# One filler product ahead of the scores in the first steps of each attention stage

## The reference, cut to what matters

```python
logits = jnp.einsum('bqhe,bkhe->bhqk', q, k) * (dh ** -0.5) + bias
p = jax.nn.softmax(jnp.where(mask, logits, -inf), axis=-1)
o = jnp.einsum('bhqk,bkhe->bqhe', p, v)
```

## Time and profile before

| | |
|---|---|
| median of 3 runs | 2877.5 us (2838.91, 2877.5, 2881.47) |
| profiled execution, its own time | 2876.28 us |
| its span, first to last instruction | 2874.5 us |
| TensorE busy | 86% of the span |
| mean granted TensorE clock | 0.888 of full speed |

### The profile page before, as it was taken

One profiled execution on the slowest core, in us unless ns is written; L12 is line 12 of the kernel. 1 busy time (PEld: TensorE's weight loads), 2 busy tenths in 40 slices (PEclk: granted clock), 3 DMA queues, 4 the chain that ended last, 5 costly groups with the idle time before them and its releaser, 6 DMA issues. The chain is left out here.

```text
span 2874.5 us, 31094 instructions
## 1 busy us (share of the span) xinstructions
PE 2486.3 (86%) x11173; PEld 1916.7 (67%) x11173; DVE 1060.6 (37%) x2010; ACT 949.1 (33%) x1428; POOL 349.4 (12%) x367
## 2 busy tenths in 40 slices
PE   4797786998689989689999789977996998799999
PEld 2586574566378868478878578933554786588877
DVE  4835522343454432332222312175335333322222
ACT  1222111333345532244421222274235332344311
POOL 0001310221022210011100000022123000111100
PEclk6897885989889999899999899886588999899999
DMA  7850001002023323033332232101001332133321
GB/s 265 268 145 15 1 1 38 5 23 59 29 85 96 96 85 90 29 88 95 95 97 79 63 90 82 49 4 44 1 30 30 88 99 76 59 95 96 112 83 67
DMA packets 347878, 212.18 MB, mean 74 GB/s; under 512 B 20252, under 2 KB 327122, under 8 KB 347757
## 3 DMA queue, kind: packets, MB, share of 16 engines
q1 hardware_dynamic: 342848, 202.64, 23.9%
q10 hardware_dynamic: 4942, 8.43, 0.8%
HBM read 208.35 MB, written 9.24 MB: 76 GB/s over the span
## 5 line engine op out<-in xcount | busy, mean ns | idle before, releaser
L220 PE MATMUL ffn_up_psum<-ffn_h_hi,ffn_up_w_hi 128*128 128x512 f32 x704 | 275.8, 392 | 35.3 <-DVE ffn_up_w_lo L299 35.3
L221 PE MATMUL ffn_up_psum<-ffn_h_lo,ffn_up_w_hi 128*128 128x512 f32 x704 | 275.3, 391 | 0.0
L222 PE MATMUL ffn_up_psum<-ffn_h_hi,ffn_up_w_lo 128*128 128x512 f32 x704 | 275.2, 391 | 0.0
L299 DVE TENSOR_TENSOR ffn_up_w_lo<-ffn_up_raw,ffn_up_w_hi 128x1024 fp32r<-128x1024 f32 x88 | 107.7, 1226 | 340.4 <-ACT ffn_up_w_hi L295 340.4
L220 PEld LDWEIGHTS ffn_up_psum<-ffn_h_hi,ffn_up_w_hi 128*128 128x128 f32 x704 | 133.2, 189 | 64.5 <-DVE ffn_up_w_lo L299 37.0
L295 ACT ACTIVATE ffn_up_w_hi<-ffn_up_raw 128x1024 fp32r<-128x1024 f32 x88 | 93.1, 1060 | 198.9 <-PE ffn_up_psum L222 195.9
L220 PE MATMUL conv_up_psum<-h_hi,conv_up_w_hi 128*128 128x512 f32 x352 | 137.9, 392 | 22.1 <-DVE conv_up_w_lo L299 22.1
L221 PEld LDWEIGHTS ffn_up_psum<-ffn_h_lo,ffn_up_w_hi 128*128 128x128 f32 x704 | 133.2, 189 | 27.8
L222 PEld LDWEIGHTS ffn_up_psum<-ffn_h_hi,ffn_up_w_lo 128*128 128x128 f32 x704 | 133.0, 189 | 27.7
L220 PE MATMUL ffn_down_psum<-ffn_hidden_hi,ffn_down_w_hi 128*128 128x512 f32 x352 | 139.4, 396 | 13.2 <-DVE ffn_down_w_lo L299 13.2
L221 PE MATMUL ffn_down_psum<-ffn_hidden_lo,ffn_down_w_hi 128*128 128x512 f32 x352 | 138.7, 394 | 0.0
(11 more groups left out here) (581 smaller groups left out, 5567.9 us busy)
## 6 DMA issues: line engine op xcount, KB each, us to landing
conv_up_raw<-in_ffn_up_dram SPq DMA_DIRECT2D x44, 512.0 KB, 3.7
ffn_up_raw<-in_ffn_w_gate_dram SPq DMA_DIRECT2D x44, 512.0 KB, 3.7
ffn_up_raw<-in_ffn_w_up_dram SPq DMA_DIRECT2D x44, 512.0 KB, 3.7
ffn_down_raw<-in_ffn_w_down_dram SPq DMA_DIRECT2D x32, 704.0 KB, 4.5
in_a_mod_slots<-in_ada_w_dram SPq DMA_DIRECT2D x16, 1024.0 KB, 6.7
branches_raw<-in_w_in_dram SPq DMA_DIRECT2D x24, 512.0 KB, 3.6
down_raw<-in_ffn_down_dram SPq DMA_DIRECT2D x16, 704.0 KB, 4.7
mod_slots<-in_ada_w_dram SPq DMA_DIRECT2D x4, 2048.0 KB, 14.0
```

The costliest lines, as they stand in the source:

```text
L220: pe.matmul(out, w_hi, r_hi, start=start, stop=False)
L221: pe.matmul(out, w_hi, r_lo, start=False, stop=False)
L222: return pe.matmul(out, w_lo, r_hi, start=False, stop=stop)
L299: dve.tensor_tensor(self.lo[:, j % PAIRS], self.raw[:, j], self.hi[:, j % PAIRS].bitcast(F32), ALU.subtract)\
```

## The change

In every step from the fifth on (i of 4 or more) and below `weigh_lag` + 2, PE gets one more product after its wait for the bias and ahead of the score. It multiplies the identity with the first columns of the constant matrices, writes them to the bank that the score is about to fill, and nobody reads them. In fox, nsa, sel and diff these are steps 4 to 8, five products a stage; in dil they are steps 4 to 10, seven. That makes 27. The first four steps have none.

```diff
+def filler_columns(score):
+
+    keys = 0 if score is None or score.coarse else score.keys
+    lacking = 0.85 * max(600 + 0.95 * keys, 750 + 0.8 * keys) - max(60, 2 * keys / 2.4)
+    return min(int(lacking * 2.4 / 4) // 32 * 32, T // 2)
+
...
                     u, c, x = pieces[i]
                     if i >= 4:
                         pe.wait_ge(biased, i - 3)
+                        filler = filler_columns(x)
+                        if i < weigh_lag + 2:
+                            pe.matmul(psum[:, i % 4, 0:filler], attention.ident,
+                                      flat(attention.square[:, 0:TT])[:, 0:filler], start=True, stop=True)
                     cols = slice(x.lo * P, x.lo * P + x.keys)
```

## The result

| | runs | median us | lowest to highest |
|---|---|---|---|
| changed kernel | 4 | 2911.74 | 2895.37 to 2918.14 |
| kernel before, beside it | 4 | 2860.01 | 2838.91 to 2881.47 |

The ratio is 1.019, with a 95% interval of 1.0119 to 1.0261: slower, by 1.2 to 2.6%. 2839 us was forecast. The profiled execution took 2895.37 us, its span is 2893.6.

A forecast was written before the change was run, and what follows sets the result against it. PE was taken to bound every attention stage, so a clock fall costs nearly its full length; 2876.3 + 6.8 (fox, sel, diff) + 3.8 (nsa) - 47.6 (dil) = 2839 us, range 2822 to 2853, or 2822 to 2889 with rivals.

The forecast's parts named there:

- The base: Starting time of the sum: the profiled execution of the kernel before, 2876.3 us, with dil's mean clock at 0.55.
- dil, the front: Dil's steps 4 to 10: seven fillers cut the 2.00 us wait for POOL to 0.4, costing +1.5 us.
- dil, the clock: Dil from its first transposes: if the full clock holds, 55.1 us gained less 6 of new waits, 49.1 us.
- Rival B: Dil: clock held at the front, lost at the first, second or third slot's end; 2863 us, chance 0.17.
- nsa: Nsa: five fillers at half clock, 4.6 us less 0.80 of wait, +3.8 us; ends +1 and 6.0.
- fox, sel, diff: These three stages: all 15 fillers on PE's path at 0.46 us each, less 0.15: +6.8 us, ends 0 and +9.0.
- A: Rival in dil: the clock falls at the stage's start all the same; 2889 us, chance 0.20.
- C: Rival in dil: transposes don't hold the clock, which falls near 1980; 2885 us, chance 0.03.

The follow-up runs named there:

- before_again: The kernel before, unchanged, run again for a second profile: median 2841.77 us against 2841.84 for the kernel before on the same chip.
- the lean kernel: Kernel before plus ten wide fillers in dil alone, in steps 4 to 7 and two at each of three slots' ends: 2833.89 us, ratio 0.990 to 0.998.
- the longer start: Kernel before without fillers, but with four warm-up products instead of three in nsa: median 2852.95 us against 2841.30.
- nsa_step8_only: Kernel before plus one filler, in step 8 of nsa: median 2913.60 us against 2841.30, with nsa at 151.9 us in its profile.
- fox_sel_diff: Kernel before plus the change's 15 fillers in fox, sel and diff alone: median 2850.50 us against 2841.84.

## Why the prediction was wrong

*The size of it.* The profiled run lies 56.1 us over the sum: 37.6 in dil, 13.9 in nsa, 2.5 in fox, sel and diff, 2.1 outside these stages. The median lies 16.4 higher still.

*The base.* The sum started from 2876.3 us, a run whose dil was at half clock for 126 us. Before's usual run has 31 us of it (13.7 and 17.1), and a median of 2841.8. I had seen 2838.91 among three runs, and wrote that a dil that kept its clock would explain it; before_again's profile, at 2838.07, shows just that, but I gave it no weight in the sum. This didn't put the number off; it hid that most runs of before had little left to gain. The gain open in dil was 144.0 - 99.9 = 44 us from the profiled run and only 7 from the usual one.

*dil, the front*: right. 2.00 us became 0.45 (0.4 was said), and the clock didn't fall there, in any of the five profiles with wide fillers at dil's front; it fell at 10.6 to 10.7 us in all eight without fillers there. One reading was wrong: I put the second wait of the earlier trace rows, 0.7 us, beside the fillers of steps 8 to 10. It stands at dil's end, at 2099.53.

*dil, the clock*: the largest error, wrong in its condition "if it holds". 49.1 us were counted on a clock that holds to dil's end. It held for 34.1 us and was then at half for 92.2, so that dil gained 10.0 in all where 47.6 was forecast. Rival B (0.17) came true at the first of its three places: the fall at 2022.96, just behind the wait of 0.64 at the slot's end. The size was about right: with the clock held dil is 99.9 to 102.9, 41 to 44 us less than 144.0. New waits take 6.6 us in the lean kernel and 6 were put down, but that is luck: I charged them to POOL at every unit's end, and it is 1.6 us for POOL in two waits and 5.0 for ACT's copies in seven.

*nsa*: the step that failed without a rival. "+3.8 us" priced the fillers and left the return where it was, but for a sooner one. The stage was at half clock for 34 us more, which with the fillers' own length cost 17.7, three times the upper end of 6.0. I took the return at 603.6 for something that the stage's work brings about on its own; it was one lucky place, and the longer start shows that even 0.85 us destroys it. B alone would have given 2876, inside the range; with nsa's late return on top the time left it.

*fox, sel, diff*: right that all 15 lie on the path. The term was mis-sized: 0.46 each was said, and 0.58 (by the median) to 0.62 (by the stages' lengths) measured, at the upper end of 0.6. The diff row that I used has equal products back to back; the filler stands between unlike ones. That the load of the weights makes the difference is likely and not shown. ACT isn't free for half of the time in diff, as I wrote: it is busy for 28.28 of 54 us. Nothing came of that.

*A* (0.20) didn't happen in the profiled run. The three other runs of the changed kernel took 2905.66 to 2918.14, 10 to 23 us over it, and have no profile; which stage took these stays open. An nsa of 151.9 us, as with the one filler in step 8, in place of 129.0 would give 2918.3, near the two slowest; that is a guess. *C* is not borne out: the lean kernel's dil ran all its transposes at 1.00. The Trainium skill's advice in TensorE: Matmul & The Clock Gate, "Why this matters for your kernels", is to leave no idle gap of some microseconds between matmul bursts. The traces don't follow the length of the gap: the clock fell behind waits of 0.64 and 0.66 us and held through waits of 1.1 us in the lean kernel.

## What to carry to other kernels

Where a stage's clock can settle in two ways, take several profiles before costing an edit, and cost it against the usual one. Any delay, even of useless work, moves everything behind it, and a return of the clock that came by luck may not come again; so guard the places where PE's work is thin (a wait, a run of small products) and no others, and read the granted clock of every stage behind the edit. In fox, sel and diff, where PE was already full, the fillers bought nothing and cost their length. A place that is thin loses the clock in some runs and not in others, so one profile that held is no proof.

## What was not expected of the hardware

The places of the clock's changes are far steadier than its outcomes. In the fourteen profiles, with dil's start anywhere from 1958.2 to 1999.4 us, the clock rose 3.8 to 3.9 us after it; in nsa it fell 7.6 to 7.8 us after the start. Yet before's two profiles, whose dil had its first fall at 10.7 us and the same products behind it, went apart at 24.4 us: one came back to 2.4 GHz, the other stayed at 1.2 GHz for 126 us, in which PE waited for 1.3: the second half of the 2.00 of the earlier trace rows, and 0.34 for ACT ahead of 1977.29.

A hint lies in the small differences. Of the eight profiles without fillers at dil's front, those whose clock rose 3.80, 3.83 and 3.85 us after dil's start (nsa_step8_only, fox_sel_diff, before) stayed at 1.2 GHz. The five that rose at 3.86 to 3.91 came back at 24.3 to 24.4 us. The order is complete, but the nearest two differ by less than 0.01 us, and no run was made to test it.
